# Differential attention: VectorE's multiplication of an older pair moves between a softmax factor and the combination of the two softmaxes

## The reference

```python
def diff_attention_mixer(h, w_in, lam, norm_g, w_out, pos, layer):
    ...
        sc = jnp.einsum('bhcqd,bhckd->bhcqk', qb, k).astype(jnp.float32) * scale
        mask = (s0 + jnp.arange(Q_BLOCK))[:, None] >= kpos[None, :]
        p = masked_softmax(sc, mask)
        attn = p[:, :, 0] - lmb * p[:, :, 1]
        return jnp.einsum('bhqk,bhkd->bqhd', attn.astype(v.dtype), v)
    ...
    o = rms_norm(o, norm_g) * (1.0 - lam_init)
    return o.reshape(b, s, D_MODEL).astype(h.dtype) @ w_out
```

## Time and profile before

| | us |
|---|---|
| median of 3 runs (lowest, highest) | 2342.19 (2340.47, 2342.29) |
| time of the profiled execution | 2342.88 |
| its span, first to last instruction | 2341.1 |
| busy PE / DVE / ACT / POOL | 2300.6 / 1780.9 / 1452.0 / 92.0 |
| mean granted TensorE clock | 0.996 of full |

### The profile page before, as it was taken

The page is one execution under the profiler, slowest core; times in us unless marked ns, Lnnn a source line. Parts: engine busy times, 40 slices in busy tenths (PEclk is TensorE's granted clock), DMA queues, the critical chain, the costliest instruction groups (busy, mean ns, idle before and its releaser), DMA issues.

```text
span 2341.1 us, 29867 instructions
## 1 busy us (share of the span) xinstructions
PE 2300.6 (98%) x11056; PEld 1909.7 (82%) x11056; DVE 1780.9 (76%) x1708; ACT 1452.0 (62%) x1572; POOL 92.0 (4%) x115
## 2 busy tenths in 40 slices
PE   8999999989999999999999999999999999999998
PEld 7888887877888888888888888888787888888887
DVE  5676445768899989898998989898796566666656
ACT  5644444457777777777777777777575446664445
POOL 0000000007200000000000000000001000000000
PEclk9999999999999999999999999999999999999999
DMA  8206654439999999999999999999512555424552
GB/s 318 92 28 208 216 180 167 148 123 347 383 368 368 367 366 365 376 356 376 354 376 356 378 353 386 327 385 338 175 64 84 206 214 196 164 73 153 200 183 85
DMA packets 268134, 597.07 MB, mean 255 GB/s; under 512 B 10245, under 2 KB 41729, under 8 KB 267392
## 3 DMA queue, kind: packets, MB, share of 16 engines
q1 hardware_dynamic: 264080, 582.01, 68.9%
q0 software_dynamic: 3920, 13.66, 1.6%
q10 hardware_dynamic: 32, 0.02, 0.0%
HBM read 591.43 MB, written 4.19 MB: 254 GB/s over the span
## 4 chain that ended last, share of the span: by engine, by line
PE 91%; DVE 5%; ACT 2%; issue 1%; DMA 0%; SPq 0%; DVEq 0%; ACTq 0%
PE up L2792 10%; PE up L2799 10%; PE up L2796 10%; PE up L2351 6%; PE up L2357 6%; PE up L2352 6%; PE acc L3092 5%; PE acc L2831 5%; PE acc L2835 5%; PE acc L2838 5%; PE acc L3097 2%; PE tp L3059 2%; PE up L3059 2%; DVE arena L2015 2%; PE acc L2497 2%; PE tp L2818 1%
## 5 line engine op out<-in xcount | busy, mean ns | idle before, releaser
L1890 DVE TENSOR_TENSOR wl<-raw,wh 128x2048 fp32r<-128x2048 f32 x378 | 865.5, 2292 | 108.2 <-ACT wh L1140 106.1
L1140 ACT ACTIVATE wh<-raw 128x2048 fp32r<-128x2048 f32 x378 | 727.3, 1924 | 202.9 <-PE up L2799 107.2
L1556 DVE TENSOR_TENSOR wl<-raw,wh 128x2048 fp32r<-128x2048 f32 x168 | 384.4, 2292 | 273.3 <-ACT wh L879 272.1
L879 ACT ACTIVATE wh<-raw 128x2048 fp32r<-128x2048 f32 x168 | 322.0, 1918 | 281.1 <-PE up L2357 107.1
L2792 PE MATMUL up<-wh,xT 128*128 128x512 f32 x1008 | 277.1, 397 | 0.0
L2799 PE MATMUL up<-wl,xT 128*128 128x512 f32 x1008 | 270.0, 390 | 0.0
L2796 PE MATMUL up<-wh,xT 128*128 128x512 f32 x1008 | 269.8, 389 | 0.0
L2351 PE MATMUL up<-wh,xT 128*128 128x512 f32 (+1 forms) x640 | 254.1, 397 | 5.6 <-DVE xT L1570 2.5
L2352 PE MATMUL up<-wh,xT 128*128 128x512 f32 (+1 forms) x640 | 249.6, 390 | 0.0
L2796 PEld LDWEIGHTS up<-wh,xT 128*128 128x128 f32 x1008 | 189.2, 188 | 40.3
L2799 PEld LDWEIGHTS up<-wl,xT 128*128 128x128 f32 x1008 | 189.2, 188 | 40.0
(11 more groups left out here) (455 smaller groups left out, 2985.5 us busy)
## 6 DMA issues: line engine op xcount, KB each, us to landing
raw<-in_moe_w_gate SPq DMA_DIRECT2D x126, 1024.0 KB, 6.8
raw<-in_moe_w_up SPq DMA_DIRECT2D x126, 1024.0 KB, 7.1
raw<-in_moe_w_down SPq DMA_DIRECT2D x126, 1024.0 KB, 6.2
raw<-in_ffn_w SPq DMA_DIRECT2D x64, 1024.0 KB, 5.6
raw<-in_hg_w_in SPq DMA_DIRECT2D x15, 1024.0 KB, 13.4
raw<-in_da_w_in SPq DMA_DIRECT2D x12, 1024.0 KB, 6.0
raw<-in_ffn_w_gate SPq DMA_DIRECT2D x22, 512.0 KB, 6.1
raw<-in_ffn_w_up SPq DMA_DIRECT2D x22, 512.0 KB, 7.4
```

The source lines that it names most:

```text
L1140: f(wh[:, x % SPLITS, :], raw[:, x % RAW, :], ACT.Copy).then_inc(moe["hi"], 1)
L1556: V.tensor_tensor(wl[:, q % SPLITS, :], raw_half(q), wh[:, q % SPLITS, :].bitcast(F32), ALU.subtract).then_inc(s_lo, 1)
L1890: V.tensor_tensor(wl[:, x % SPLITS, :], raw[:, x % RAW, :], wh[:, x % SPLITS, :].bitcast(F32), ALU.subtract).then_inc(moe["lo"], 1)
```

## The change

In DVE's loop, the combination L1841 of pair n-1 moves behind L1847 of pair n-3. The factor's instruction L1838 is now only marked instead of linked, and the combination waits for it (`behind`) after L1847 and its wait for `at_sq` have gone ahead. Operands, sizes and the number of vector instructions stay as they are.

```diff
                 link(V.reciprocal(a[:, 4:6], a[:, 2:4]))
-                link(V.tensor_scalar(a[:, 5:6], a[:, 5:6], nlam, a[:, 2:3], ALU.mult, ALU.mult))
-                if m >= 2:
-                    dve.wait_ge(at_T, m - 1)
-                V.scalar_tensor_tensor(stage[:, m % 2, 0:w], at_p[:, m % 2, 1, 0:w], a[:, 5:6], at_p[:, m % 2, 0, 0:w],
-                                       ALU.mult, ALU.add).then_inc(at_w, 1)
+                scaled_sum = mark(V.tensor_scalar(a[:, 5:6], a[:, 5:6], nlam, a[:, 2:3], ALU.mult, ALU.mult))
             if 3 <= n:
                 m = n - 3
                 j, b = m // NB, m % NB
                 dve.wait_ge(at_sq, m + 1)
                 V.scalar_tensor_tensor(o[:, b, j * P:(j + 1) * P], acc[:, m % 2, 0:P], att[:, m % 4, 4:5], gn[:, :],
                                        ALU.mult, ALU.mult).then_inc(at_og, 1)
+            if 1 <= n <= NA:
+                m = n - 1
+                w = P * (m % NB + 1)
+                behind(scaled_sum)
+                if m >= 2:
+                    dve.wait_ge(at_T, m - 1)
+                V.scalar_tensor_tensor(stage[:, m % 2, 0:w], at_p[:, m % 2, 1, 0:w], att[:, m % 4, 5:6], at_p[:, m % 2, 0, 0:w],
+                                       ALU.mult, ALU.add).then_inc(at_w, 1)
```

## The result

| | before | after |
|---|---|---|
| median of 6 runs each (lowest, highest), us | 2341.74 (2340.47, 2342.29) | 2349.05 (2346.10, 2352.32) |
| ratio, with its 95% interval | | 1.0030 (1.0019 to 1.0041) |
| time and span of the profiled execution, us | 2342.88, 2341.1 | 2347.03, 2345.2 |

The change makes the kernel slower by 7.3 us by the medians, 4.4 to 9.6 us by the interval. The six runs of the kernel before spread over only 1.8 us, but that was few runs: in the two later comparisons 25 runs of it spread over 7.4 us and 18 over 6.6. The profiled execution of the changed kernel is one of its shorter ones, so a single pair of traces can't be read by its total. I read the attention first, then follow the offset between the two traces to the end.

A forecast was written before the change was run, and what follows sets the result against it. A DVE-PE ring bounds the attention; a longer one through the square was to replace it, 4.03 us per round for 3.32. Six rounds plus pair 15 delay it 5.1 us, from median 2342.19 to 2347.3 us, range 2345.2 to 2350.6.

The forecast's parts named there:

- The ring of the earlier trace: First attention before the change: two-pair round through DVE and PE, by odd maximum, combination, transposition, product and scores, 3.32 us.
- the one forecast: New ring in the attention: combination, transposition, product, square, multiplication, next combination; 4.03 us per round instead of 3.32.
- The even-to-odd step: Attention loop, from an even combination to the next odd one: 1.98 us instead of 1.36.
- The odd-to-even step: Attention loop, from an odd combination to the next even one, through ACT's copy and square: 2.05 us instead of 1.96.
- DVE's saving of 0.12 us per pair: DVE's queue: unlinked L1847 starts 0.19 behind the factor instead of 0.31; rival that this wins, 2340.5 us, chance 0.03.
- The stall: DVE ahead of L1847: stands still about 0.45 us for an odd pair's square; an even pair's wait is just met.
- The order of VectorE's starts: DVE: combination 0.26 behind L1847's start by the trace, 0.35 by the skill, which would make the sum 6.3 us.
- Pass-through: Behind the attention: the shift passes through; rival that some 2 us are given back, 2345.3 us, chance 0.09.
- a rival of 3.4 us inside the ring: TensorE's clock falls to half for two rounds of the attention, 3.4 us more: 2350.7 us, chance 0.12.
- Two of its own signs of being wrong: Forecast is wrong if the granted clock leaves 1.00 between 469 and 502, or the span grows less than the attention.
- the sentence that behind pair 15 nothing changes: Loop's end: L1847 of pairs 14 and 15 have no combination behind them, so the attention ends 5.1 us later.
- The sum: Whole attention: six rounds of 4.03 us, then 1.98 for pair 15, 5.1 us later in all; bounds 4.6 to 6.3.

The follow-up runs named there:

- the older pair: Changed kernel, but the multiplication between factor and combination is that of pair n-4 instead of n-3; 2343.71 us, ratio 1.0012.
- the kept-busy kernel: Changed kernel with five small products of constants on PE in each of the loop's last two gaps; 2347.41 us, ratio 1.0022.
- the factor linked: Changed kernel with the factor's instruction linked again instead of marked; 2354.57 us in a single execution.
- more work on ACT: Two small copies added on ACT ahead of each pair's square; single executions 2353.12 us in the changed kernel, 2341.84 in the kernel before.
- even only: Kernel before with the new order only in front of the combinations of even pairs; 2343.1 us, ratio 1.0006.
- odd only: Kernel before with the new order only in front of the combinations of odd pairs; 2345.19 us, ratio 1.0015.

## Why the prediction was right, and where it was off

- **What bounds the attention.** Right. The ring of the earlier trace rows gave way to the one forecast. DVE waits for the square ahead of each multiplication, and PE now waits for the odd pairs' combination too, 0.35 us.
- **The even-to-odd step.** 1.98 forecast from four rows, 1.98 measured. The rows taken from the loop's end, where engines run dry, were the right ones for an instruction that an idle engine waits for: in the full loop none could be seen.
- **The odd-to-even step.** 2.05 forecast, 2.04 measured. The steps are met one by one, within 0.02 us: 0.53, 0.47, 0.28, 0.49 and 0.27 for 0.55, 0.47, 0.28, 0.49 and 0.26. The round is 4.03 against 4.02, the delay of pair 15 5.09 against 5.01.
- **DVE's saving of 0.12 us per pair.** Right in size (0.19 from factor to multiplication) and right in being worth nothing: with the older pair in its place it turns into idle before the odd maximum.
- **The stall.** I wrote of 0.45 us for odd pairs, and of a square just in time for even ones. In the closed ring it is 0.59 and 0.32. The 0.45 was read from the kernel before; in the new round everything moves, and only the sum round the ring, not the single stall, could be trusted.
- **The order of VectorE's starts.** The combination starts 0.27 behind the multiplication, while the latter takes 0.35. The section of the Trainium skill ("VectorE: DVE Perf Modes", "The DRAIN you can't avoid") has the next operation wait until the pipeline is empty, and adds that one which is not held starts earlier. The trace agrees with the addition, which the prediction left out. That a semaphore costs nothing the runs don't bear out: behind the same factor the next instruction starts after 0.31 us with a link and after 0.19 without.
- **Pass-through.** Right as far as the experts' end: the 6.6 us at their start are 6.7 there, so nothing is given back on the way. Behind that the offset moves where the clock falls in one trace and not in the other.
- **The clock.** This is the term that was missing. I held a fall for a rival of 3.4 us inside the ring. It came on top of the forecast, at the place where the scores run out, and costs 1.25 us in this pair of traces. The rival's row had the right sign: gaps, then the lower level when the work is back. I applied it to the ring's gaps, of 0.35 and 0.68 us, which left the clock at 1.00 in all three traces of this order, and not to the last two, which grow from 1.11 and 0.65 us to 1.25 and 1.33. The Trainium skill ("TensorE: Matmul & The Clock Gate", "What's actually happening") sets the gate by how busy the engine has been; the kept-busy kernel agrees in its one trace.
- **Two of its own signs of being wrong came true.** The granted clock left 1.00 between 469 and 502 us (0.51 from 500), and the span of the profiled pair grew by less than the attention, by 4.1 us against 6.3. Both come from falls of the clock, at the loop's end and in the later stages, and not from the ring. The part on the ring stands; the sentence that behind pair 15 nothing changes does not.
- **The noise.** The prediction took 0.9 us to either side from three runs. Of 25 single executions of the kernel before, the farthest lies 4.85 us from their median. The medians of the changed kernel, 2349.05 and 2348.05, lie within the range forecast; one of its single executions, 2352.32, does not.
- **The sum.** With the clock it is 5.0 + 1.25 = 6.3 us, 2348.0 from the median of 2341.74. The two comparisons gave 7.3 and 5.4 us, on either side of it. That the forecast's 2347.3 came within 1.7 us is in part luck: it started from a median of three runs, 0.45 above that of six, which hides about a third of the missing term. The chance of 0.64 for slower by over 0.2% was fair by the forecast alone and low with the missing term.

## What to carry to other kernels

When an instruction that needs another engine's late result moves ahead of one that feeds that engine, follow the dependence once round all queues: a stall that looks like 0.45 us can close a ring whose length is the sum of all its steps. Take the steps of such a ring from where the engines already wait for each other, at the start or end of a loop, and look at the ends of the loop once more, where the engines run dry and the clock may fall. If a filler is wanted between two linked instructions, take one whose inputs are ready one iteration earlier; and check first that the queue it fills is the one that others wait for.

## What the runs showed of the hardware

- Two waits ahead of one VectorE instruction delay it by 0.06 us if the later of them is the one that releases it: 0.09 us from the square's end to the start instead of 0.03, at each of five pairs followed in the one trace with the factor linked. Where both are satisfied early, behind a running instruction, they show no cost.
- On VectorE an unlinked instruction starts before the former has ended: 0.19 us behind the start of one that takes 0.27, and 0.27 behind one that takes 0.35. A link behind the first makes it 0.31.
- A fall of TensorE's clock at the end of this loop costs 1.1 to 1.6 us, read from six traces with and four without it. It came in the six with a gap of 1.24 to 1.43 us ahead of pair 14's transposition, and not in the four with 1.11, 1.11, 0.83 and none there; that this gap is the cause is not shown.
- Which of the later gaps of the program draw a fall differs between kernels whose code there is the same. The kernel before, its trace with more work on ACT, and those with the older pair, even only, odd only and the factor linked have it in the second attention. The two traces of the changed kernel, the one with its end kept busy and the one with more work on ACT have it in the convolution instead.
- Such falls are of the size of the effect studied here, so a total from one execution says little at this level. The mean granted clock of an execution tells much of it. Of the 25 executions of the kernel before, ten had 0.998 and took 2339.9 us in the mean, eleven had 0.997 and 2341.6, three had 0.996 and 2344.6, and one had 0.995 and 2346.2.
